# Writing the feed-forward convolution's new state from SBUF element by element during the FFN, in place of transposed row stores at the end

## What is computed

```python
def conv_ffn(h, prefix, w_up, conv_w, conv_b, w_down):
    up = h @ w_up
    T = up.shape[1]
    ext = jnp.concatenate([prefix.astype(up.dtype), up], axis=1)
    c = conv_b + sum(ext[:, j:j + T] * conv_w[j] for j in range(CONV_WIDTH))
    gate, val = jnp.split(c, 2, axis=-1)
    return (jax.nn.gelu(gate) * val) @ w_down, ext[:, -(CONV_WIDTH - 1):]
...
x = x + rms_norm(f, g_ffn_post)
```

## Time and profile before

| | |
|---|---|
| time, median of 3 runs | 1866.5 us (1866.03 to 1866.72) |
| time of the profiled execution | 1863.46 us |
| span in the profile | 1861.7 us |
| mean granted TensorE clock | 0.997 |
| PE busy | 1813.8 us, 97% |
| DVE busy | 871.5 us, 47% |
| ACT busy | 524.3 us, 28% |
| POOL busy | 263.4 us, 14% |
| DMA packets | 162282, 113.73 MB |

### The profile page before, as it was taken

One profiled execution on the slowest core, in us unless ns is written; L12 is line 12 of the kernel. 1 busy time (PEld: TensorE's weight loads), 2 busy tenths in 40 slices (PEclk: granted clock), 3 DMA queues, 4 the chain that ended last, 5 costly groups with the idle time before them and its releaser, 6 DMA issues.

```text
span 1861.7 us, 28851 instructions
## 1 busy us (share of the span) xinstructions
PE 1813.8 (97%) x11113; PEld 1722.9 (93%) x11113; DVE 871.5 (47%) x1111; ACT 524.3 (28%) x838; POOL 263.4 (14%) x309
## 2 busy tenths in 40 slices
PE   6999999999999999999999999999999999999998
PEld 5878787879699899999999889999999999999997
DVE  5565757475244432222342576552145552455536
ACT  4575747481100100000023452221012210122224
POOL 1121212120133211101101000000001001000002
PEclk9999999999999999999999999999999999999999
DMA  5202020205411111111132121111111111111312
GB/s 166 69 24 68 23 68 23 68 14 178 124 41 51 34 51 45 53 42 41 51 126 68 35 115 55 45 45 46 45 45 45 44 45 47 46 51 49 131 30 97
DMA packets 162282, 113.73 MB, mean 61 GB/s; under 512 B 5389, under 2 KB 152213, under 8 KB 161947
## 3 DMA queue, kind: packets, MB, share of 16 engines
q1 hardware_dynamic: 161035, 108.34, 19.4%
q10 hardware_dynamic: 1200, 4.75, 0.7%
HBM read 95.86 MB, written 13.40 MB: 59 GB/s over the span
## 4 chain that ended last, share of the span: by engine, by line
PE 88%; ACT 5%; DVE 3%; issue 2%; DMA 1%; SPq 0%; ACTq 0%; POOL 0%; DVEq 0%; POOLq 0%
PE ps L1462 67%; PE ps L1472 9%; PE misc L1554 3%; PE misc L1448 1%; ACT zl L728 1%; ACT zl L733 1%; PE ps L1728 1%; PE ps L1786 1%; PE ps L1538 1%; PE misc L1746 1%; ACT att L745 1%; PE ps L1448 1%; PE ps L1539 1%; PE ps L1542 1%; PE ps L1544 1%
## 5 line engine op out<-in xcount | busy, mean ns | idle before, releaser
L1462 PE MATMUL ps<-h_hi,w_lo 128*128 128x344 f32 x1896 | 403.6, 321 | 3.2 <-DVE w_lo L1061 2.4
L1462 PE MATMUL ps<-h_lo,w_hi 128*128 128x344 f32 x1896 | 402.4, 320 | 0.0
L1462 PE MATMUL ps<-h_hi,w_hi 128*128 128x344 f32 x1896 | 400.3, 319 | 0.0
L1061 DVE TENSOR_TENSOR w_lo<-stage,w_hi 128x1024 fp32r<-128x1024 f32 x148 | 198.6, 1342 | 337.9 <-POOL w_hi L561 337.0
L561 POOL TENSOR_SCALAR w_hi<-stage 128x1024 fp32r<-128x1024 f32 x148 | 158.6, 1071 | 1304.3 <-PE ps L1462 1062.3
L1462 PEld LDWEIGHTS ps<-h_hi,w_lo 128*128 128x128 f32 x1896 | 318.8, 188 | 5.6 <-issue 4.2
L1462 PEld LDWEIGHTS ps<-h_lo,w_hi 128*128 128x128 f32 x1896 | 320.8, 189 | 0.0
L1462 PEld LDWEIGHTS ps<-h_hi,w_hi 128*128 128x128 f32 x1896 | 315.9, 188 | 0.0
L1472 PE MATMUL ps<-h_hi,w_lo 128*128 128x344 f32 x408 | 137.1, 336 | 0.0
L1338 DVE TENSOR_TENSOR up<-ps,work 128x1032 f32<-128x1032 f32 x44 | 54.2, 1232 | 171.9 <-PE ps L1462 165.4
L1472 PE MATMUL ps<-h_lo,w_hi 128*128 128x344 f32 x408 | 131.2, 322 | 0.0
(11 more groups left out here) (268 smaller groups left out, 2567.3 us busy)
## 6 DMA issues: line engine op xcount, KB each, us to landing
stage<-in_w_in SPq DMA_DIRECT2D x48, 512.0 KB, 3.8
stage<-in_w_up SPq DMA_DIRECT2D x44, 512.0 KB, 3.7
stage<-in_w_down SPq DMA_DIRECT2D x16, 448.0 KB, 3.2
stage<-in_w_branch SPq DMA_DIRECT2D x24, 256.0 KB, 2.6
x_scratch<-trunk SPq DMA_DIRECT2D x1, 4128.0 KB, 11.2
x_back<-x_scratch SPq DMA_DIRECT2D x1, 4128.0 KB, 12.8
x_tok<-in_x_prompt SPq DMA_DIRECT2D x8, 512.0 KB, 8.1
kv_pg<-in_cache_k SPq DMA_DIRECT2D x16, 256.0 KB, 3.8
```

The source lines that it names most:

```text
L1061: V.tensor_tensor(w_lo[par][:, :, :], stage[par][:, :, :], w_hi[par][:, :, :].bitcast(F32), ALU.subtract).then_inc(w_lo_made, 1)
L1462: last = M(ps[par][:, c, :], w[par][:, k, :], x[:, c * CH:(c + 1) * CH], start=(k == 0 and s == 0), stop=(k == n - 1 and s == 2))
```

## The change

The two outputs are viewed by feature tile: partition p of tile f is feature 128 f + p. In each of the FFN's 22 pairs, behind the copy to `g_hi`, ACT's queue waits for its own two copies to `tails` and issues four DMAs, two for each k: 128 partitions x 2 elements to `conv_prompt` and 128 x 8 elements to `conv_sample`. In DRAM, elements of one partition lie a whole row apart, and neighbouring partitions lie 4 bytes apart. `tail_rows`, `conv_rows_out` and SP's 22 row stores are removed, with the waits that belonged to them. The final wait of SP counts the 88 new DMAs. Each tile has ten columns of its own in `tails`, as before.

```diff
-        ROW_GROUPS = 2 * FT // 4
-        ROWS_AFTER = [range(min(2 * n + 1, ROW_GROUPS), min(2 * n + 3, ROW_GROUPS)) for n in range(len(F_PARTS))]
+        tail_p_v = conv_prompt[0, 0, :, :].rearrange("t (f p) -> p f t", p=P)
+        tail_s_v = conv_sample[0, :, 1, :].rearrange("b (f p) -> p f b", p=P)
...
-            for n in range(2 * FT // 4):
-                sp.wait_ge(tail_sb, n + 1)
-                rows = up[n % 2][0:TAIL, 0:4 * P]
-                sp.dma_start(conv_prompt[0, 0, :, n * 4 * P:(n + 1) * 4 * P], rows[0:2, :]).then_inc(tail_out[n % 2], 16)
-                sp.dma_start(conv_sample[0, :, 1, n * 4 * P:(n + 1) * 4 * P], rows[2:TAIL, :]).then_inc(tail_out[n % 2], 16)
...
-                sp.wait_ge(tail_out[k], 32 * ((2 * FT // 4 + 1 - k) // 2))
+                sp.wait_ge(tail_out[k], 16 * 2 * FT)
...
-                        A(tails[:, f, :].rearrange("p o t -> p (o t)"), up[k][:, T - TAIL:T], ACT.Copy)
+                        A(tails[:, f, :].rearrange("p o t -> p (o t)"), up[k][:, T - TAIL:T], ACT.Copy
+                          ).then_inc(tail_sb, 1)
...
+                    act.wait_ge(tail_sb, j * 2 + 2 * (f0 + 1))
+                    for k in range(2):
+                        f = bass.ds(j + (f0 + k * FT), 1)
+                        tail = tails[:, f, :].rearrange("p o t -> p (o t)")
+                        act.dma_start(tail_p_v[:, f, :].rearrange("p o t -> p (o t)"), tail[:, 0:2],
+                                      allow_slow_non_contiguous=True).then_inc(tail_out[0], 16)
+                        act.dma_start(tail_s_v[:, f, :].rearrange("p o b -> p (o b)"), tail[:, 2:TAIL],
+                                      allow_slow_non_contiguous=True).then_inc(tail_out[1], 16)
...
-            def conv_rows_out(first, end):
-                for n in range(first, min(end, ROW_GROUPS)):
-                    act.wait_ge(tail_ps, n + 1)
-                    if n >= 2:
-                        act.wait_ge(tail_out[n % 2], 32 * (n // 2))
-                    A(up[n % 2][0:TAIL, 0:4 * P], misc[0:TAIL, (n % 2) * 512:(n % 2) * 512 + 4 * P], ACT.Copy
-                      ).then_inc(tail_sb, 1)
...
-            def tail_rows(r):
-                if r >= 2:
-                    pe.wait_ge(tail_sb, r - 1)
-                for j in range(4):
-                    t = T_(misc[0:TAIL, (r % 2) * 512 + j * P:(r % 2) * 512 + (j + 1) * P], tails[:, 4 * r + j, :])
-                t.then_inc(tail_ps, 1)
...
-            tail_rows(0)
...
-                for r in ROWS_AFTER[n]:
-                    tail_rows(r)
-            pe.wait_ge(tail_sb, ROW_GROUPS)
```

More of the change, by code:

```diff
@@ L1021, in y_out @@
                 A(y_tok[:, n % 4, :], yt_buf[n], ACT.Copy).then_inc(yt_left, 1)
-            conv_rows_out(0, 1)
             f_square(0)
-            conv_rows_out(1, 3)
             f_square(1)
-            conv_rows_out(3, 5)
             f_square(2)
             rstd_f(0)
-            conv_rows_out(5, 7)
             f_square(3)
-            conv_rows_out(7, 9)
             f_square(4)
@@ L1035, in _ @@
             rstd_f(1)
-            conv_rows_out(9, 11)
             y_out(0)
```

## The result

| | before | after |
|---|---|---|
| median | 1866.26 us (1860.56 to 1866.72, 4 runs) | 1889.95 us (1887.77 to 1896.32, 4 runs) |
| ratio | | 1.0136, 95% interval 1.0121 to 1.0151 |
| span in the profile | 1861.7 us | 1886.0 us |

The kernel became slower by 1.36%, where the forecast was 2.2 us faster and the range ended at 1871.5. The page of the changed kernel, busy time, then the two queues of the DMA (packets, MB, share of 16 engines): q1 is SP's, q10 is ACT's.

The account below looks back on a forecast made before the run. PE was taken to bound the kernel up to its third part at the end, DVE after it. Transposes -2.18 us and all else 0 gave 1866.5 - 2.2 = 1864.3 us, range 1861.7 to 1871.5.

Parts of the forecast that it names:

- the transposes: End of the kernel: removing 44 transposes saves 4.8 us of PE, of which only 2.18 us shortens the chain.
- The 2.18 us ahead of the hand-over: Before the chain passes from PE to DVE: 20 transposes removed move it up by 2.18 us.
- the other 24 transposes: Behind the hand-over to DVE: 2.6 us of PE work beside DVE's own work, removal worth nothing.
- ACT's copies and SP's stores: End of the kernel: removing ACT's 11 copies and SP's 22 row stores, value 0, hidden by DVE's work.
- the issues: ACT's queue in each FFN pair: four issues take 1.5 to 3.0 us, inside ACT's 4.49 us gap.
- Rival 2: Ends of groups: ACT's issues stall and PE waits longer for `g_lo`; 1873.3 us, chance 0.14.
- a packet: DMA queue in each pair: 69 ns for each element packet, 11.3 us an engine, fitting in 19.0 us.
- rival 3: DMA queue in the FFN pairs: too slow altogether from 116 ns a packet; about 1987 us at 150 ns, chance 0.09.
- the sentence on the weights: Weight loads in the pairs: one element packet ahead of each weight packet adds 4.4 us, still 12 us early.
- the term of the sum for all that the packets do: FFN pairs: cost of the element stores to the total time, taken as 0.
- Rival 4, the clock: End of the kernel: PE idles 2.1 us, its clock falls earlier, the last part is 1.7 us late; 1866.0 us, chance 0.15.
- The estimate of 1.7 us for a drain: DMA queue: at about 10.5 ns a packet a pair's elements drain in 1.7 us, so ACT could not stall.

## Why the prediction was wrong

**Right: the transposes.** The 2.18 us ahead of the hand-over came as worked out, and the other 24 transposes brought nothing. The run without stores and POOL's account of the changed kernel both give 2.2. ACT's copies and SP's stores were priced at nothing, and are worth little: from the hand-over on, the run without stores is 0.5 us shorter than the kernel before.

**Right: the issues.** 0.39 us each as a rule, inside the 4.49 us gap, one packet for each element. Only in the last pair one issue took 9.18 us; the table load and squares of the last down projection waited behind it. Rival 2 (ACT's issues stall) fell; its place, PE's wait for `g_lo` at the ends of groups, did not grow.

**Mis-sized, on the safe side: a packet.** I took 69 ns from the row stores; an element packet takes 8 ns to SBUF or to a place of its own, and 22 on average in the changed kernel. So rival 3, an overloaded queue at 116 ns and more, fell too: q10 used 5.0% of the engines over the span.

**The step that failed.** It is the sentence on the weights: "if each of its 64 packets an engine had one element packet ahead of it, 4.4 us more". I let the elements cost the weights only while both stood on the engines, and so the term of the sum for all that the packets do was 0. It measured 26 us (1889.95 - 1866.26 + 2.2). In the trace the elements' packets had ended, and each weight packet still took 156 ns, while the stores were not yet reported complete. The disturbance outlives the recorded packets; it lies on the DRAM side, since the same packets to SBUF don't cause it, and depends on where the elements land. My bounds all came from durations of the packets themselves, so none could hold it. A row that shows how the next reads fare behind such stores was not in the trace of before; I should have said that this price was unknown to above and put a rival on it.

**And PE.** All rivals reached the end through weights, ACT or PE's waits. In fact most of the loss of the changed kernel, up to 18.9 us, is PE stopping inside a unit with its operands ready (13.6 us), with its report of the unit before coming late, and the half clock behind it. These halts occur only in runs whose weight packets are slow (81 ns and up), never at 55 and below; not every such run has them in its trace (none at 95 ns). What PE lacks is not shown by any row. A late load of instructions doesn't fit: none is recorded at the first three halts, and it would not explain why a unit's report, due at 1194.15, came at 1202.39 when PE went on with the next unit until 1198.7. PE's reports and the DMAs' increments come late together in the changed kernel, which suggests something that both need. In the run with padded rows three of nine halts have no such increment at their end, and no run tests it. The cause of the halts stays open. `x1_back`, 6.3 us of the loss, does not occur in the prediction at all.

**Rival 4, the clock.** Without stores PE idled 2.3 us ahead of the mean-square product (2.1 forecast), but its clock stayed up; it fell only at 1843 us, where it falls before at 1847. In the profiled execution with elements alone and rows far apart it did fall there, at 1835.4 for 3.4 us behind an idle stretch of 2.27, and cost nothing: DVE took the last part 15.98 us after the hand-over, against 15.99 in the run without stores. So the event of this rival can happen and its 1.7 us did not. The half clock that costs in the changed kernel is another: behind the halts and behind the wait for `x1_back`.

**The Trainium skill's rule.** The Trainium skill's advice against a strided last dimension ("DMA: Bandwidth & Descriptors", "Rules for kernel authors") pointed the right way. Its reason, one descriptor for each element, is seen in 58,928 packets, but that number of descriptors cost nothing where the elements lay alone. What costs here is where they land. The estimate of 1.7 us for a drain took the Trainium skill's 10.5 ns a packet wrongly: the same page's measured bandwidth has it for the 64 packets of one whole load, and I multiplied it by the packets of one engine. The last packet record ends 4.2 us after a pair's first issue in the run to SBUF, and 11.0 us in the changed kernel.

## What to carry to other kernels

Price a store by what it does to the reads behind it, not only by its own packets: compare the mean duration of untouched packets (here 28 against 83 ns) before looking for waits. Elements of 4 bytes that are neighbours in DRAM should not be written one by one from many partitions while weights stream in, least of all into rows far apart; the same count to SBUF or to 64-byte places cost nothing here. And before work is moved off the end of a kernel, see which engine has the chain there: only 20 of 44 transposes counted, and moving them behind the hand-over kept 1.4 of the 2.2 us in the trace, less than the median can tell from no change.

## What was not expected of the hardware

- 2560 elements of 4 bytes, written as neighbours into ten rows, slow a 512 KB load whose packets start after theirs have ended from 2 us to 14; the stores' own increments come up to 22 us after the first issue (median), 11 us after the last packet.
- A fifth of the elements costs no time, and all of them in bursts of half the length still 16 us: it isn't in proportion.
- Two scratch layouts with nearly the same pitch (45,056 and 45,568 bytes) differ by 19 us, and the outputs, with the pitch of the first, lie between them. What in the placement decides is open.
- PE can stop in the middle of a unit for up to 4.3 us with no wait in the program, while DVE and POOL receive its report of the unit before 8 us late, and goes on within 0.17 us of the next increment by a DMA.
- PE's clock fell to half behind a 2.4 us wait at 1101 us in some executions and stayed up behind the same wait in others.
